# Moving the gate product of a PEER layer from VectorE's one-hot matrices to GpSimd

## The reference

```
def peer_ffn(x, w_query, sub_keys, down, up):
    q = (xt @ w_query).reshape(T, H, 2, PEER_HALF)
    s = jnp.einsum('thcd,cnd->thcn', q, sub_keys)
    sv, si = lax.top_k(s, K)
    cand_s = (sv[:, :, 0, :, None] + sv[:, :, 1, None, :]).reshape(T, H, K * K)
    cand_i = (si[:, :, 0, :, None] * PEER_NKEYS + si[:, :, 1, None, :]).reshape(T, H, K * K)
    top_s, pos = lax.top_k(cand_s, K)
    idx = jnp.take_along_axis(cand_i, pos, axis=-1)
    gate = jax.nn.softmax(top_s, axis=-1)
    a = jnp.einsum('thkd,td->thk', down[idx], x)
    c = gate * jax.nn.gelu(a)
    return jnp.einsum('thk,thkd->td', c, up[idx])
```

## Time and profile before

| what | us |
|---|---|
| median of 3 runs | 2626.51 |
| lowest and highest | 2623.84, 2628.50 |
| profiled execution, its own time | 2628.5 |
| its span, first to last instruction | 2626.7 |
| mean granted TensorE clock | 0.973 |
| PE busy in the span | 2463.5 |
| DVE busy | 1713.2 |
| ACT busy | 1195.2 |
| POOL busy | 878.6 |
| gate stretches | about 1017 to 1262 and 2025 to 2270 from the span's start |

### The profile page before, as it was taken

The page is one execution under the profiler, slowest core; times in us unless marked ns, Lnnn a source line. Parts: engine busy times, 40 slices in busy tenths (PEclk is TensorE's granted clock), DMA queues, the critical chain, the costliest instruction groups (busy, mean ns, idle before and its releaser), DMA issues.

```text
span 2626.7 us, 40337 instructions
## 1 busy us (share of the span) xinstructions
PE 2463.5 (94%) x16347; PEld 2252.5 (86%) x16347; DVE 1713.2 (65%) x3065; ACT 1195.2 (46%) x1801; POOL 878.6 (33%) x406
## 2 busy tenths in 40 slices
PE   4998878997899999999999999798999999999999
PEld 4997868987788999999888887687999999988887
DVE  6776956546564877899644444655777899744444
ACT  4444554444444444443444444354444443444443
POOL 3112522114334663000344443343665000144443
PEclk9998999998999999999999999899999999999999
DMA  7886634664234454444555555234545444555554
GB/s 271 325 289 243 233 104 143 210 201 141 87 114 166 166 176 154 137 145 137 188 194 195 193 192 173 97 113 147 170 159 172 143 145 137 169 194 193 194 195 161
DMA packets 126587, 457.44 MB, mean 174 GB/s; under 512 B 13973, under 2 KB 16961, under 8 KB 125634
## 3 DMA queue, kind: packets, MB, share of 16 engines
q1 hardware_dynamic: 121442, 441.52, 49.8%
q10 hardware_dynamic: 4048, 8.91, 0.9%
q0 software_dynamic: 912, 4.42, 0.5%
HBM read 451.62 MB, written 5.93 MB: 174 GB/s over the span
## 4 chain that ended last, share of the span: by engine, by line
PE 80%; DVE 14%; ACT 3%; issue 2%; DMA 1%; POOL 0%; SPq 0%; ACTq 0%; DVEq 0%; POOLq 0%
PE bank L610 24%; PE bank L611 24%; PE bank L612 24%; PE bank L1173 4%; DVE sb L1882 1%; DVE sb L1829 1%; ACT sb L1216 1%; DVE sb L2421 1%; DVE sb L2578 1%; DVE sb L2574 1%; DVE sb L1844 1%; PE bank L1149 1%; DVE sb L2581 0%; PE bank L977 0%; DMA sb<-in_w_ada_dram 0%
## 5 line engine op out<-in xcount | busy, mean ns | idle before, releaser
L610 PE MATMUL bank<-sb,sb 128*128 128x256 f32 (+1 forms) x4744 | 1529.1, 322 | 38.1 <-DVE sb L1829 28.9
L611 PE MATMUL bank<-sb,sb 128*128 128x256 f32 (+1 forms) x4744 | 1502.2, 317 | 0.0
L612 PE MATMUL bank<-sb,sb 128*128 128x256 f32 (+1 forms) x4744 | 1501.4, 316 | 0.0
L2686 POOL TENSOR_TENSOR sb<-sb,sb 128x1024 fp32r<-128x1024 f32 x325 | 816.0, 2514 | 1514.9 <-ACT sb L1216 1514.8
L1216 ACT ACTIVATE sb<-sb 128x1024 fp32r<-128x1024 f32 x765 | 808.0, 1058 | 1089.7 <-PE bank L612 1085.2
L610 PEld LDWEIGHTS bank<-sb,sb 128*128 128x128 f32 x4744 | 916.6, 193 | 106.2 <-issue 24.0
L611 PEld LDWEIGHTS bank<-sb,sb 128*128 128x128 f32 x4744 | 916.9, 193 | 56.3 <-issue 1.8
L612 PEld LDWEIGHTS bank<-sb,sb 128*128 128x128 f32 x4744 | 915.4, 193 | 56.0
L1829 DVE TENSOR_TENSOR sb<-sb,sb 128x1024 fp32r<-128x1024 f32 x440 | 547.8, 1245 | 598.4 <-ACT sb L1216 597.2
L2650 DVE TENSOR_TENSOR sb<-sb,sb 128x1024 fp32r<-128x1024 f32 x64 | 160.0, 2499 | 150.1 <-ACT sb L1785 150.1
L2613 DVE TENSOR_SCALAR sb<-sb,sb 128x128 f32<-128x128 f32 x512 | 142.2, 341 | 0.0
(11 more groups left out here) (273 smaller groups left out, 1351.7 us busy)
## 6 DMA issues: line engine op xcount, KB each, us to landing
sb<-in_peer_down_dram SPq DMA_DIRECT2D x256, 512.0 KB, 3.3
sb<-in_peer_up_dram SPq DMA_DIRECT2D x256, 512.0 KB, 3.3
sb<-in_w_ada_dram SPq DMA_DIRECT2D x72, 512.0 KB, 5.9
sb<-in_hyb_in_dram SPq DMA_DIRECT2D x56, 512.0 KB, 3.3
sb<-in_ffn_gate_dram SPq DMA_DIRECT2D x44, 512.0 KB, 4.2
sb<-in_ffn_up_dram SPq DMA_DIRECT2D x44, 512.0 KB, 4.6
sb<-in_ffn_down_dram SPq DMA_DIRECT2D x44, 512.0 KB, 4.2
sb<-in_mix_in_dram SPq DMA_DIRECT2D x25, 512.0 KB, 4.4
```

The costliest lines, as they stand in the source:

```text
L610: e.matmul(out, a[0], b[0], start=start, stop=False)
L611: e.matmul(out, a[0], b[1], start=False, stop=False)
L612: return e.matmul(out, a[1], b[0], start=False, stop=stop)
L2686: self.e.tensor_tensor(rr(M.lo[k % NSPLIT]), M.raw[k % NRAW], M.hi[k % NSPLIT], ALU.subtract).then_inc(*self.S.tick("lo_pool", k))
```

## The change

The change has four parts. (1) `LOWS` gives every third low part of the PEER tiles 73 to 136 to POOL. (2) `o1` is now a plain one-hot matrix, made by one tensor_tensor compare, in place of four tensor_scalar instructions. (3) The gate is multiplied into `o2` by a new POOL instruction for each group, in place, with the gate broadcast along 128 elements; PE's `gate_product` waits for it as well. On POOL's queue it stands ahead of the low part of tile r+3. (4) Both `store` functions, on ACT and on DVE, walk their operands with the token outermost and the key innermost; before, the four tokens were innermost. The number of elements is the same.

```
--- before.py
+++ after.py
@@ -44,7 +44,7 @@
     "mix1": ((3, ("pool",)), (28, ("pool", "pool", "dve", "pool")), (33, ("dve",))),
     "ffn2": ((3, ("pool",)), (63, ("dve", "dve", "dve", "dve", "dve", "pool")), (66, ("dve",))),
     "hyb": ((3, ("pool",)), (33, ("dve", "pool", "pool")), (36, ("dve",))),
-    "peer": ((3, ("pool",)), (11, ("dve", "pool")), (73, ("pool", "pool", "pool", "dve")), (137, ("dve",)),
+    "peer": ((3, ("pool",)), (11, ("dve", "pool")), (73, ("pool", "pool", "pool", "dve")), (137, ("dve", "dve", "pool")),
              (261, ("dve", "pool")), (264, ("dve",))),
 }
 
@@ -1169,6 +1169,7 @@
         bank = self.take()
         self.K.bank["gates", self.s, g] = bank
         self.wait_ge("one_hot1", self.s, g)
+        self.wait_ge("gated", self.s, g)
         for j in range(4):
             x = self.e.matmul(bank[:, 128 * j:128 * (j + 1)], m.o2[g % 2][:, j], m.o1[g % 2][:, j], start=True, stop=True)
         x.then_inc(*self.S.tick("gates", self.s, g))
@@ -1736,10 +1737,10 @@
 
         def store(g):
             k = 64 + 8 * (g // 8)
-            c = m.C[:, :, 4 * g:4 * g + 4]
-            bank = self.K.bank["gates", s, g].rearrange("p (t n) -> p n t", t=4)
+            c = m.C[:, :, 4 * g:4 * g + 4].rearrange("p n t -> p t n")
+            bank = self.K.bank["gates", s, g].rearrange("p (t n) -> p t n", t=4)
             self.wait_ge("gates", s, g)
-            self.e.activation(c[:, k:], bank[:, k:], AF.Copy).then_inc(*self.S.tick("gates_copy", s, g))
+            self.e.activation(c[:, :, k:], bank[:, :, k:], AF.Copy).then_inc(*self.S.tick("gates_copy", s, g))
 
         for i in range(64):
             if i >= 3:
@@ -2608,20 +2609,17 @@
                 self.wait_ge("gates", s, g - 2)
             e.tensor_tensor(o2, iota, m.keep[:, 2, 4 * g:4 * g + 4].unsqueeze(2).to_broadcast(wide), ALU.is_equal).then_inc(
                 *self.S.tick("one_hot2", s, g))
-            for j in range(4):
-                t = 4 * g + j
-                x = e.tensor_scalar(o1[:, j], M.const("iota"), m.keep[:, 1, t:t + 1], m.keep[:, 0, t:t + 1], op0=ALU.is_equal,
-                                    op1=ALU.mult)
-            x.then_inc(*self.S.tick("one_hot1", s, g))
+            e.tensor_tensor(o1, iota, m.keep[:, 1, 4 * g:4 * g + 4].unsqueeze(2).to_broadcast(wide), ALU.is_equal).then_inc(
+                *self.S.tick("one_hot1", s, g))
 
         def store(g):
             b = g // 8
             k = 64 + 8 * b
-            bank = self.K.bank["gates", s, g].rearrange("p (t n) -> p n t", t=4)
-            c = m.C[:, :, 4 * g:4 * g + 4]
+            bank = self.K.bank["gates", s, g].rearrange("p (t n) -> p t n", t=4)
+            c = m.C[:, :, 4 * g:4 * g + 4].rearrange("p n t -> p t n")
             self.wait_ge("gates_copy", s, g)
             self.wait_ge("gelu", s, k - 2)
-            e.tensor_tensor(c[:, 0:k], bank[:, 0:k], c[:, 0:k], ALU.mult).then_inc(*self.S.tick("gates_put", s, g))
+            e.tensor_tensor(c[:, :, 0:k], bank[:, :, 0:k], c[:, :, 0:k], ALU.mult).then_inc(*self.S.tick("gates_put", s, g))
             if g % 8 == 7:
                 n = 126 if b == 7 else k + 8
                 c = m.C[:, k:n, 32 * b:32 * b + 32]
@@ -2878,9 +2876,19 @@
 
 
 
+    def gates(self):
+        m, s = self.m, self.s
+        for g in range(64):
+            o2 = m.o2[g % 2]
+            self.wait_ge("one_hot2", s, g)
+            self.e.tensor_tensor(o2, o2, m.keep[:, 0, 4 * g:4 * g + 4].unsqueeze(2).to_broadcast([128, 4, 128]), ALU.mult).then_inc(
+                *self.S.tick("gated", s, g))
+            yield
+
     def peer(self, l):
         self.features()
         self.linear(8)
+        self.tasks = {"gates": self.gates()}
         for n in range(0, 128, 2):
             if n == 62:
                 self.ahead_first = False
```

## The result

| | us |
|---|---|
| before, median of 4 runs | 2626.98 |
| after, median of 4 runs (2691.18 to 2693.84) | 2692.11 |
| ratio, with its 95% interval | 1.025 (1.0232 to 1.0268) |

The account below looks back on a forecast made before the run. PE's pace of 3.765 us a tile was taken as the bound; turns of DVE and POOL make it 4.15, 25 us a stretch less 5 of lead, 40 in all: 2666, range 2638 to 2708.

Parts of the forecast that it names:

- A gate stretch is set by PE's pace alone.: Gate stretches before the change: PE busy 240 of 240 us, 3.765 us a tile; lightening DVE or ACT wins nothing.
- DVE and POOL take turns and become the bound.: Gate stretches: sharing the SBUF port makes a tile 4.15 us against PE's 3.765; 40 us in all, chance 0.50.
- An instruction of DVE with one input does not take turns.: DVE beside POOL: one-input instructions run without waiting for POOL, as L2581 did in 2.29 us for 2048 elements.
- The product's hold: Gate stretches: time POOL's gate product holds the port against DVE, 0.93 to 1.15 us, taken as 1.04.
- The lead of 5 us is used up once in each stretch.: DVE's low parts run ahead of PE, absorbing 5 of a stretch's 25 us of lateness; 20 us a stretch stay.
- the sum for three tiles: DVE with POOL in the gate stretches: 3.76 + 8.16 + 3 x (0.14 + 0.04) = 12.46 us, 4.15 a tile.
- I take the lower end, because L2624 is the nearest row.: Store's new SBUF walk: assumed unchanged at 1.04 ns an element, the upper end being 2.08.
- Rival 1: Strided store is slow: 0.38 us more a store, 33 us on top of the 40, 2700 in all; chance 0.27.
- Edits at nothing: Costed at zero: PE's added wait on POOL's product, ACT's store, the gate's move to o2, SP's loads 1.2 us later.
- Rival 2: Gate stretches: the turns fit and nothing changes, 2626.5, if a product holds DVE up by 0.73 us; chance 0.11.
- Rival 3: Key searches: a lighter DVE ends PE's 6.5 us waits for low parts in each, 2613.5 at best; chance 0.05.
- Rival 4: Gate stretches: the product holds DVE up by only 0.85 us, so 16 us are lost, 2642; chance 0.07.

Follow-up runs that it names:

- e9: Kernel before with the plain compare for o1 and the gate product made by ACT, one gates step later in its queue; 2632.9 us, ratio 1.0018.
- e10: Kernel before with o1 and o2 written and multiplied in rounded fp32r form for PE's gate product; 2586.9 us, ratio 0.9845.
- e1_old_walk: The whole change, but both store functions keep the old walk with four tokens innermost; 2663.2 us, ratio 1.0132 against the kernel before.
- e4: Kernel before with only the LOWS table changed, every third low part of the gate stretches on POOL; 2635.2 us, ratio 1.0028.
- e7: The whole change, but ACT's store keeps the old walk and only DVE's is strided; 2694.4 us, ratio 1.0243 against the kernel before.
- e3: Kernel before with only the plain compare for o1, POOL's product and PE's wait on it; old walk, DVE's low parts; 2641.5 us, ratio 1.0052.
- e12: e1_old_walk with one thing moved: DVE does store(g-3) behind the two compares, not ahead; 2631.9 us, ratio 1.0018 against the kernel before.
- e2: Kernel before with only the new walk in both store functions, POOL idle in the gate stretches; 2648.9 us, ratio 1.0084.

## Why the prediction held, and where it was off

- **"A gate stretch is set by PE's pace alone."** Right, and shown from the other side too: e9 takes 0.5 us a tile from DVE and its steps stay at 3.767 us, e10 takes 0.45 us from PE and gains 21 us a stretch.
- **DVE and POOL take turns and become the bound.** Right, with a limit: in the full change DVE is full or nearly so, and POOL's lost turns add waits that the sum doesn't have. The compare that meets POOL's low part was forecast near 3 us and took 2.85, the low part behind a product near 2 and took 2.06. The forecast for the turns alone was 2666.5; e1_old_walk, which is just that, took 2663.2.
- **"An instruction of DVE with one input does not take turns."** Wrong as a rule. It was read from a TENSOR_REDUCE; the TENSOR_SCALAR L2613 waits for POOL in e4. My own rows had it: L2417, a TENSOR_SCALAR too, ends at 742.93, 0.16 us after POOL's low part (740.36, 2.41 us). The forecast doesn't hang on it, since the change takes L2613 out of DVE's list.
- **The product's hold, 0.93 to 1.15 us, taken at 1.04.** It measured 0.89 to 0.91, the lower end. The row with the broadcast factor was the right one.
- **"The lead of 5 us is used up once in each stretch."** Near in size, but at the wrong wait, and a term is missing. With a hold of 0.93 the sum for three tiles is 12.46 - 0.33 = 12.13, 4.04 us a tile, 17.8 us a stretch over PE's pace. In e1 the 62 steps of a stretch lost 13.8 us, so some 4 us were absorbed. PE waits at the gate product, not at a low part. And PE's added wait, counted at nothing because "PE takes it a tile later", is not nothing for the last product, which PE wants at once: it starts 3.75 us behind the one before in e1, where it was 1.24. Over both stretches the hold makes it 14 us less, the lead 2 more and the last product 5 more: 40 - 14 + 2 + 5 = 33, against 34 in the stretches and 36.5 between the medians. That the forecast for the turns came within 3 us of e1 is in part luck, two errors against each other.
- **"I take the lower end, because L2624 is the nearest row."** This is the step that failed. The store measured 2.30 ns an element, above even my upper end of 2.08. The walk is worth 28.9 us in the full change (e1 against after) and 22 us alone. Rival 1, to which I gave 0.27, had it at 33 us and 2700 in all, on top of the turns, and that is what came true. The measured time lies in the range because the range took rival 1 in, and not because 2666 was near. The row that I followed tells of a step in PSUM, and the price is SBUF's.
- **Edits at nothing.** ACT's store: right (e7). PE's added wait: 1.9 us a stretch by itself (e9), and it is the place where the lateness shows. SP's later loads: right, PE waits for no load in the first stretch.
- **Rival 2, "no change".** Its point of decision, a hold of 0.73 us, was not reached: e3, with the product alone, lost 15 us. What I held against it, that DVE's next instruction after `o1` needs the port, is what e12 took away, and with it the time came near rival 2's.
- **Rival 3, "faster".** No sign of it: PE's waits for DVE's low parts on L610 are 27.3 us and were 28.9.
- **Rival 4, "a smaller loss".** The hold came near its 0.85 us, but DVE had no idle time left to hide it in: e1 has DVE busy for 198.8 of 200 us.
- **"Outside the gate stretches nothing should move."** Right: 32 us twice are 64 of the 65. A stretch was to grow by 20 us and grew by 32.

All my sums go by the mean of a stretch. The store grows through it, so DVE's load does too, and in e2, e3 and e4 the lateness is nearly all in the second half and at the last product.

## What to carry to other kernels

Moving work from DVE to POOL is no relief where both then read SBUF with two operands (or DVE does a TENSOR_SCALAR): they take whole instructions in turn, and what counts is the sum of both and which instruction stands behind the one that POOL waits for. Put an instruction that doesn't need the port there; one line moved gave back 31 of 36 us. Ask first which engine's pace sets the stretch: here it was PE, and only work taken from PE made it shorter. Where an engine's load grows through a stretch, compare its heaviest part and not its mean with the pace, and look at the last step, which has nothing behind which to hide. And keep at least two fp32 neighbours innermost in SBUF; a strided side in PSUM cost nothing.

## What the runs showed of the hardware that I had not expected

- DVE with one fp32 element at each step of 1 KB in SBUF, read and written, ran at 2.30 ns an element, more than twice the 1.04 ns of four side by side. ACT, which only writes such a walk, took 635 ns for 256 elements, 400 with two side by side and 378 with four. How DVE's extra time is shared between its read and its write was not run.
- The port is not given strictly to the one that waited first: in the full change POOL's product of 1205.93 waited through a compare, a low part and `put`, 2.96 us, while in e1_old_walk, e3_product_alone and e12_store_behind none of 128 took more than 1.5 us. With the new walk in DVE's store 18 of 128 did (the full change and e7). What links the two stays open.
